# Hybrid attention and MoE block on one core: the first forgetting head's keys, queries and values loaded inside the sliding attention, and five of eight output-weight pieces loaded inside the last forgetting head

## What is computed

```python
def reference(x, meta, ...):
    h = layer_norm(concatenate([meta, x]), ln_in_g, ln_in_b)        # 16 + 2048 tokens, 1024 wide
    proj = h @ w_in                                                 # q,k,v of both head groups, forget gates
    qa, ka, va, qb, kb, vb, fb = split(proj, sizes)
    log_f = log_sigmoid(fb + b_f)
    o_a = sliding_sink_attention(qa, ka, va, sinks, rel_bias, ...)  # 8 heads, 2 key heads, chunks of 64
    o_b = forgetting_attention(qb, kb, vb, log_f, ...)              # 8 heads, causal, bias from cumsum(log_f)
    mix = concatenate([o_a, o_b]) @ w_o
    h = layer_norm(alpha * h + mix, ln1_g, ln1_b)
    h = layer_norm(alpha * h + hierarchical_moe(h, ...), ln2_g, ln2_b)
    return h[:, N_META:]

def forgetting_attention(q, k, v, log_f, key_valid):
    cum = cumsum(log_f)
    for i in blocks of 128 queries:
        s = q_i @ k[:hi].T * HEAD_DIM ** -0.5 + cum_i - cum_keys
        p = softmax(where(causal mask, s, -inf))
        o_i = p @ v[:hi]
```

## Time and profile before

| | us |
|---|---|
| median of three runs | 2511.67 (2507.01 to 2515.30) |
| the profiled execution, its own time | 2511.47 |
| the profiled execution, span from first to last instruction | 2509.5 |
| granted clock of PE, mean over the span | 0.938 of full |
| input projection, from the start to about | 499 |
| sliding attention, about 503 to | 689 |
| forgetting attention, about 695 to | 1267 |
| output projection, from about | 1272 |

### The profile page before, as it was taken

One profiled execution on the slowest core, in us unless ns is written; L12 is line 12 of the kernel. 1 busy time (PEld: TensorE's weight loads), 2 busy tenths in 40 slices (PEclk: granted clock), 3 DMA queues, 4 the chain that ended last, 5 costly groups with the idle time before them and its releaser, 6 DMA issues. The chain is left out here.

```text
span 2509.5 us, 35865 instructions
## 1 busy us (share of the span) xinstructions
PE 2196.5 (88%) x11294; PEld 1790.3 (71%) x11294; DVE 1707.6 (68%) x3144; ACT 1491.3 (59%) x2261; POOL 330.4 (13%) x438
## 2 busy tenths in 40 slices
PE   7999899858859999999979994699999999999970
PEld 6778788645547777777858883587888888788860
DVE  5323231167668888888743334899999999899976
ACT  4323241256557767777633331587888888788856
POOL 0111111110000000000000000122222222222211
PEclk9999999969979999999989996799999999999985
DMA  6525352253252222220043331899787869999837
GB/s 196 175 101 152 126 178 87 76 133 88 64 132 60 66 68 66 68 68 9 8 165 144 142 125 51 294 374 328 240 261 238 281 228 340 325 301 303 270 79 285
DMA packets 213834, 420.06 MB, mean 167 GB/s; under 512 B 42920, under 2 KB 90104, under 8 KB 212824
## 3 DMA queue, kind: packets, MB, share of 16 engines
q1 hardware_dynamic: 180680, 314.15, 36.8%
q0 software_dynamic: 32016, 103.26, 14.3%
q10 hardware_dynamic: 1032, 1.31, 0.4%
HBM read 437.12 MB, written 86.39 MB: 209 GB/s over the span
## 5 line engine op out<-in xcount | busy, mean ns | idle before, releaser
L2348 DVE TENSOR_TENSOR moe_w_lo<-fetch_w_raw,moe_w_hi 128x1024 fp32r<-128x1024 f32 x376 | 435.2, 1217 | 9.4 <-ACT moe_w_hi L2277 9.1
L2277 ACT ACTIVATE moe_w_hi<-fetch_w_raw 128x1024 fp32r<-128x1024 f32 x376 | 368.5, 1053 | 63.9 <-PEq L92 32.5
L2402 PE MATMUL moe_ps_gu<-moe_w_hi,moe_xT_hi 128*128 128x512 f32 x736 | 293.8, 399 | 3.9 <-DVE moe_xT_lo L2359 3.9
L2404 PE MATMUL moe_ps_gu<-moe_w_hi,moe_xT_lo 128*128 128x512 f32 x736 | 289.3, 393 | 0.0
L2403 PE MATMUL moe_ps_gu<-moe_w_lo,moe_xT_hi 128*128 128x512 f32 x736 | 288.7, 392 | 0.0
L1355 ACT ACTIVATE fox_p_hi<-fox_ps_t 128x512 fp32r<-128x512 f32 (+4 forms) x352 | 181.2, 531 | 108.6 <-PE fox_ps_t L1495 107.8
L1422 DVE TENSOR_TENSOR fox_p_lo<-fox_ps_t,fox_p_hi 128x512 fp32r<-128x512 f32 (+4 forms) x352 | 211.0, 611 | 28.7 <-ACT fox_p_hi L1355 27.2
L1495 PE MATMUL fox_ps_t<-ident,fox_s 128*128 128x128 f32 (+1 forms) x1216 | 200.3, 280 | 29.3 <-ACT fox_s L1348 18.4
L2354 DVE TENSOR_TENSOR moe_d_lo<-fetch_d_raw,moe_d_hi 128x1024 fp32r<-128x1024 f32 x184 | 213.1, 1220 | 10.7 <-ACT moe_d_hi L2285 7.4
L1409 DVE CUSTOM_DVE_ANT_0 fox_s<-fox_ps_r,fox_ncum 128x512 f32<-128x512 f32 (+4 forms) x352 | 193.8, 569 | 21.0 <-PE fox_ps_r L1480 13.9
L1348 ACT ACTIVATE fox_s<-fox_s,fox_ntop 128x144 f32<-128x144 f32 (+5 forms) x192 | 173.4, 904 | 46.8 <-DVE fox_ntop L1417 46.3
(11 more groups left out here) (313 smaller groups left out, 4991.4 us busy)
## 6 DMA issues: line engine op xcount, KB each, us to landing
fetch_w_raw<-in_w_e_gate_dram SPq DMA_DIRECT2D x192, 512.0 KB
fetch_w_raw<-in_w_e_up_dram SPq DMA_DIRECT2D x192, 512.0 KB
fetch_d_raw<-in_w_e_down_dram SPq DMA_DIRECT2D x92, 1024.0 KB
proj_w_raw<-in_w_in_dram SPq DMA_DIRECT2D x24, 1024.0 KB, 5.2
proj_xt<-in_x_dram SPq DMA_DIRECT2D x16, 512.0 KB
h<-proj_hrow POOLq DMA_DIRECT2D x16, 512.0 KB, 3.4
win_q_raw<-qT SPq DMA_DIRECT2D x32, 256.0 KB, 4.0
mix_o<-o SPq DMA_DIRECT2D x16, 512.0 KB, 4.4
```

The lines of the kernel that those rows point to most:

```text
L2277: nc.scalar.activation(w_hi[:, k], w_raw[:, k].rearrange("p j n -> p (j n)"), ACT.Copy).then_inc(gu_high, 1)
L2348: nc.vector.tensor_tensor(w_lo[:, k], w_raw[:, k].rearrange("p j n -> p (j n)"), w_hi[:, k].bitcast(F32), ALU.subtract).then_inc(gu_split, 1)
L2402: nc.tensor.matmul(out, xT_hi[:, slot, k], w_hi[:, k, cols], start=k == 0, stop=False)
L2404: done = nc.tensor.matmul(out, xT_lo[:, slot, k], w_hi[:, k, cols], start=False, stop=k == KT - 1)
```

## The change

A tile `raw` of 5200 floats in each partition is made once, outside the four stages, with semaphores `k_in`, `q_in`, `v_in` and `w_in` of its own. In the projection it takes the place of `w_raw` and `gain`; in the forgetting attention it is `k_raw`, `q_raw` and `v_raw`; afterwards its first 5120 floats hold pieces 0 to 4 of `w_o`. `phase_mix` has a smaller tile `w_rest` for pieces 5 to 7. The small tiles of `keep` are made earlier; the instructions on them are the same.

```diff
+RAW = TOK + SEQ + (TILES + 1) * HD
+W_AHEAD = RAW // D
+def load_head(sp, t, ahead, h):
+    k_raw, q_raw, v_raw = raw_head(ahead)
+    row, first = (A_KV + h) * HD, SBT + META
+    for i, cols in enumerate((slice(0, first), slice(first, TOK))):
+        for half in range(2):
+            sp.dma_start(k_raw[half * HD:half * HD + HD, cols], t["kT"][row:row + HD, cols]).then_inc(ahead["k_in"][i], 16)
+    row = (A_HEADS + h) * HD
+    for i, cols in enumerate((slice(0, SBT), slice(SBT, SEQ))):
+        for half in range(2):
+            sp.dma_start(q_raw[half * HD:half * HD + HD, cols], t["qT"][row:row + HD, cols]).then_inc(ahead["q_in"][i], 16)
+    cols = slice((A_KV + h) * HD, (A_KV + h + 1) * HD)
+    sp.dma_start(v_raw[:, 0:TILES], t["v"][META:TOK, cols].rearrange("(b p) d -> p b d", p=P)).then_inc(ahead["v_in"], 16)
+    sp.dma_start(v_raw[0:META, TILES], t["v"][0:META, cols]).then_inc(ahead["v_in"], 16)
...
 # phase_window, SP and POOL
             for n in range(4, TILES):
                 load_queries(n)
                 load_values(n)
+                if n == 11:
+                    sp.wait_ge(fox_zeroed, 1)
+                    load_head(sp, t, ahead, 0)
...
+            nc.gpsimd.memset(raw_head(ahead)[2][:, TILES], 0.0).then_inc(fox_zeroed, 1)
...
 # phase_forget, SP and POOL
-            load_keys(0, K_COLS[0], 0)
-            load_queries(0, Q_COLS[0], 0)
             sp.dma_start(ncum[:, 0, 0:FIRST], row_broadcast(t["ncum"][0, 0:FIRST], P)).then_inc(cum_first, 16)
-            sp.wait_ge(zeroed, 1)
-            load_values(0)
-            load_keys(0, slice(FIRST, TOK), 1)
-            load_queries(0, slice(SBT, SEQ), 1)
             sp.dma_start(ncum[:, 0, FIRST:TOK], row_broadcast(t["ncum"][0, FIRST:TOK], P)).then_inc(cum_in[0], 16)
...
+            sp.wait_ge(k_split, PIECES * B_HEADS)
+            sp.wait_ge(q_split, PIECES * B_HEADS)
+            sp.wait_ge(v_split, 2 * B_HEADS)
+            for k in range(W_AHEAD):
+                sp.dma_start(ahead["raw"][:, k * D:(k + 1) * D], t["w_o"][0, k * P:(k + 1) * P, :]).then_inc(ahead["w_in"][k], 16)
...
-            nc.gpsimd.memset(v_raw[:, TILES], 0.0).then_inc(zeroed, 1)
...
 # phase_mix, SP
-            for k in range(KT):
-                sp.dma_start(w_raw[:, k], t["w_o"][0, k * P:(k + 1) * P, :]).then_inc(w_in[k], 16)
+            for k in range(W_AHEAD, KT):
+                sp.dma_start(w_raw(k), t["w_o"][0, k * P:(k + 1) * P, :]).then_inc(w_in[k], 16)
```

More of the change, by code:

```diff
@@ L100, in row_broadcast, with phase_project @@
     return bass.AP(ap.tensor, ap.offset, [[0, parts]] + [list(x) for x in ap.ap])
-def phase_project(nc, sems, ident, t, gates):
+def phase_project(nc, sems, ident, t, gates, ahead):
     with ExitStack() as ctx:
@@ L116, in phase_project @@
         SLOTS = 6
-        gain = m.sb("gain", [P, D])
+        gain = ahead["raw"][:, 2 * KT * GW:2 * KT * GW + D]
         shift = m.sb("shift", [P, D])
@@ L129, in phase_project @@
         mT = m.sb("mT", [P, KT, 2 * META], F32R)
-        w_raw = m.sb("w_raw", [P, 2, KT * GW])
+        w_raw = ahead["raw"][:, 0:2 * KT * GW].rearrange("p (s n) -> p s n", s=2)
         w_hi = m.sb("w_hi", [P, 2, KT, GW], F32R)
@@ L686, in bucket_runs, with raw_head, phase_window @@
     return runs
-def phase_window(nc, sems, ident, t, gates):
+def raw_head(ahead):
+    raw = ahead["raw"]
+    return raw[:, 0:TOK], raw[:, TOK:TOK + SEQ], raw[:, TOK + SEQ:RAW].rearrange("p (b d) -> p b d", d=HD)
+def load_head(sp, t, ahead, h):
[11 more added lines that the diff above has]
+    sp.dma_start(v_raw[0:META, TILES], t["v"][0:META, cols]).then_inc(ahead["v_in"], 16)
+def phase_window(nc, sems, ident, t, gates, ahead):
     with ExitStack() as ctx:
@@ L744, in phase_window @@
         ones_ready = m.sem("ones_ready")
+        fox_zeroed = m.sem("fox_zeroed")
         k_in = [m.sem(f"k_in{i}") for i in range(2)]
@@ L1119, in row_pieces, with phase_forget @@
     return [(0, keys)] if keys <= 8 * P + META else [(0, half), (half, keys - half)]
-def phase_forget(nc, sems, ident, t):
+def phase_forget(nc, sems, ident, t, ahead):
     with ExitStack() as ctx:
@@ L1190, in phase_forget @@
         ps_o = m.ps("ps_o", [P, 512])
-        zeroed = m.sem("zeroed")
         future_ready = m.sem("future_ready")
@@ L1197, in phase_forget @@
         cum_in = [m.sem(f"cum_in{i}") for i in range(2)]
-        k_in = [m.sem(f"k_in{i}") for i in range(2)]
-        q_in = [m.sem(f"q_in{i}") for i in range(2)]
-        v_in = m.sem("v_in")
+        k_in, q_in, v_in = ahead["k_in"], ahead["q_in"], ahead["v_in"]
         k_high = m.sem("k_high")
@@ L1533, in _, with phase_mix @@
             turn_back(UNITS - 1)
-def phase_mix(nc, sems, ident, t, logits):
+def phase_mix(nc, sems, ident, t, logits, ahead):
     with ExitStack() as ctx:
@@ L1548, in phase_mix @@
         shift = m.sb("shift", [P, D])
-        w_raw = m.sb("w_raw", [P, KT, D])
+        w_rest = m.sb("w_rest", [P, KT - W_AHEAD, D])
         w_hi = m.sb("w_hi", [P, KT, D], F32R)
@@ L1575, in phase_mix @@
         eps_ready = m.sem("eps_ready")
-        w_in = [m.sem(f"w_in{k}") for k in range(KT)]
+        w_in = ahead["w_in"]
         w_high = m.sem("w_high")
@@ L1599, in phase_mix, with w_raw @@
         block = ctx.enter_context(nc.Block())
+        def w_raw(k):
+            return ahead["raw"][:, k * D:(k + 1) * D] if k < W_AHEAD else w_rest[:, k - W_AHEAD]
         def tiles(engine, body):
@@ L1695, in _ @@
                 act.wait_ge(w_in[k], 16)
-                nc.scalar.activation(w_hi[:, k], w_raw[:, k], ACT.Copy).then_inc(w_high, 1)
+                nc.scalar.activation(w_hi[:, k], w_raw(k), ACT.Copy).then_inc(w_high, 1)
             def body(n, slot, use):
@@ L1743, in _ @@
                 dve.wait_ge(w_high, k + 1)
-                nc.vector.tensor_tensor(w_lo[:, k], w_raw[:, k], w_hi[:, k].bitcast(F32), ALU.subtract).then_inc(w_split, 1)
+                nc.vector.tensor_tensor(w_lo[:, k], w_raw(k), w_hi[:, k].bitcast(F32), ALU.subtract).then_inc(w_split, 1)
             dve.wait_ge(norm_in, 32)
@@ L2546, in hybrid_block_kernel @@
         ident = ctx.enter_context(nc.sbuf_tensor("ident", [P, P], F32))
[L2547 to L2553, removed]
         keep = Space(nc, ctx, "keep", ctx)
@@ L2562, in hybrid_block_kernel @@
                  "more_pairs": keep.sb("more_pairs", [1, 1], I32)}
-        phase_mix(nc, ctx, ident, t, logits)
-        with ExitStack() as ahead:
-            raw = Space(nc, ahead, "fetch", ctx)
+        with ExitStack() as before:
+            early_raw = Space(nc, before, "ahead", ctx)
+            ahead = {"raw": early_raw.sb("raw", [P, RAW]),
+                     "k_in": [early_raw.pool_dma_sem(f"k_in{i}") for i in range(2)],
+                     "q_in": [early_raw.pool_dma_sem(f"q_in{i}") for i in range(2)],
+                     "v_in": early_raw.pool_dma_sem("v_in"),
+                     "w_in": [early_raw.pool_dma_sem(f"w_in{k}") for k in range(KT)]}
+            with ExitStack() as early:
+                gate_rows = Space(nc, early, "gates", ctx)
+                gates = {"forget": gate_rows.sb("forget", [B_HEADS, TOK]), "b_forget": gate_rows.sb("b_forget", [B_HEADS, 1]),
+                         "one": gate_rows.sb("one", [B_HEADS, 1])}
+                phase_project(nc, ctx, ident, t, gates, ahead)
+                phase_window(nc, ctx, ident, t, gates, ahead)
+            phase_forget(nc, ctx, ident, t, ahead)
+            phase_mix(nc, ctx, ident, t, logits, ahead)
+        with ExitStack() as fetched:
+            raw = Space(nc, fetched, "fetch", ctx)
             fetch = {"w_raw": raw.sb("w_raw", [P, KT, 2, D_EXPERT]), "d_raw": raw.sb("d_raw", [P, DT, D]),
```

4 lines of the change are left out of this document (1 added, 3 removed).

## The result

| | before | after |
|---|---|---|
| median of 20 runs each, us | 2513.18 (2507.01 to 2516.44) | 2518.57 (2511.61 to 2523.86) |
| ratio after / before | | 1.0020, 95% interval 1.0012 to 1.0029 |
| span of the profiled execution | 2509.5 | 2515.0 |
| granted clock of PE, mean | 0.938 | 0.939 |

The changed kernel is slower by 5.4 us (the interval is 3.0 to 7.3 us). The forecast was 4.8 us slower, and less than the 0.3% from which it would have called the kernel slower. Both came true.

The account below looks back on a forecast made before the run. Stages run one behind another with barriers; in the sliding attention PE is busy 27.58 of 30 us. 2511.47 + 12.7 - 7.6 - 0.3 = 2516.3 us, 2512 to 2519 from the terms' ends, range 2508 to 2522.

Parts of the forecast that it names:

- Part 1, the stall: Sliding attention: ten loads ahead of queries 12 make ACT's split of them 11.0 us late; they land at 636.5.
- the fixed 2.3: Sliding attention, in the landing time of queries 12: 2.3 us that a first small load needs beyond its bytes.
- the store's 1.1: Sliding attention, in the landing time of queries 12: 1.1 us for one 256 KB store of `o` by POOL.
- Part 1, behind the stall: Sliding attention after the stall: loop absorbs 0.3 us; PE at 1.2 GHz for 4.5 to 5 us costs 2.0 us.
- Part 2, the start of the forgetting attention: Forgetting attention's start: PE begins 3.3 us earlier, DVE's waits of 1.40 and 2.88 us go; 7.6 us saved.
- the fourth rival: Forgetting attention's start: `ncum` or a barrier takes the place of keys and queries; 3.3 us lost, 2519.6 us; chance 0.07.
- the upper end of the term: Forgetting attention's start: 9.5 us saved if PE's clock rises earlier because the gap in its work is shorter.
- Part 3, the weights: Five weight pieces loaded during head 7 cost nothing; output projection saves 0.3 us at `o` of tile 2.
- Fast transfers: Sliding attention: loads move at 412 GB/s, queries 12 are 5.2 us late; 2510.0 us; chance 0.15.
- Queries 12 beside the head: Sliding attention: queries 12 are served beside the head's loads, so the stall could vanish; 2503.6 us; chance 0.05.
- The clock that stays down: Sliding attention: PE stays at half clock for 20 us more after the stall, costing 9 us; 2525 us; chance 0.15.
- The sign on later stages: Changed profile: the forecast is wrong if the later stages differ by more than 2 us.

Follow-up runs that it names:

- e1: Changed kernel with head 0's ten loads behind the values of tile 15 instead of tile 11; 2503.73 us against 2512.20 before, ratio 0.9969.
- e4: Changed kernel with only head 0's keys behind values 11, its queries and values behind values 15; one run, 2504.19 us against 2512.20 before.
- e5: Changed kernel with head 0's keys and queries behind values 11, its values behind values 15; one run, 2506.97 us against 2513.82 before.
- e10: Changed kernel with head 0's loads on POOL's queue, behind the store of tile 6, instead of SP's; one run, 2509.61 us against 2511.89 before.
- e8: Changed kernel with head 0's loads on POOL's queue, behind the store of tile 7, instead of SP's; one run, 2512.92 us against 2513.82 before.
- e6: Changed kernel with head 0's loads between queries 12 and values 12 in SP's queue; one run, 2513.45 us against 2513.82 before.
- e7: Changed kernel with head 0's keys behind queries 11, queries behind queries 12, values behind queries 13; 2501.21 us against 2513.82 before, ratio 0.9952.
- e9: e7 with all eight output-weight pieces loaded in the output projection again; 2505.58 us against 2511.89 before, ratio 0.9976.

## Why the prediction was right, point by point

**Part 1, the stall.** Forecast 11.0 us late, measured 12.3. The mechanism was the named one, bytes in front of queries 12 (e1, e4, e5), and the term was 1.3 us too small, inside its ends. The steps of e4, e5 and after show where the 1.3 us are. At my 235 GB/s the keys, the queries and the values are 4.5, 4.5 and 2.2 us, and my other terms (the fixed 2.3 and the store's 1.1 against what queries 12 needed before) take 0.2 off; measured were 5.8, 4.6 and 1.9. So, read from one profile each, the rate was about right and the fixed part too small by 1.5 us, already with the keys alone. The hold of SP by the last value load, 6.66 us, was in no term, though the earlier trace rows has one of 5.32. Because of it queries 12 were issued 12.8 us behind the values and not the 8 to 12 forecast; no cost of it is seen, since the step with the hold in it is the one that came out cheaper than its bytes.

**Part 1, behind the stall.** Forecast -0.3 absorbed and +2.0 for the clock, so +1.7; measured 13.1 - 12.3 = +0.8. The half clock lasted 4.6 us, in the forecast's 4.5 to 5. But the next interval was only 0.93 us longer than before (9.41 against 8.48): the loop, whose tile body is not all PE work, took up more than half of what PE lost. The two errors nearly cancel, and that is luck: 12.7 forecast, 13.1 measured.

**Part 2, the start of the forgetting attention.** Forecast 7.6 us, measured 8.35 (F, 578.56 to 570.21); the nine other kernels with the head ahead have 567.8 to 572.3 in F, the two without it 578.5 and 579.9. PE's first product came 3.5 us sooner (3.3 forecast), and the two waits of DVE (4.3 us) went. The wait for `ncum` that the fourth rival named did appear, with 1.31 us, but it ended what DVE would mostly have waited for PE anyway: at DVE's first scores 3.4 us were saved. The rest of 0.7 fits the clock, which came back after 14 us of PE's work instead of 20; the upper end of the term had that, but no run isolates it.

**Part 3, the weights.** Forecast 0.3 us. In the profile 0.7 us came at tile 2's `o`, as named, and up to 1.5 us in O, of which the kernels with and without it show 0.8 on average. The chip's ratio cannot tell it from 0.

**The rivals.** Fast transfers: at 412 GB/s, by that rival's own sum, after would have been 5.2 us late and not 12.3. The Trainium skill, DMA: Bandwidth & Descriptors, section Bandwidth, gives 341 GB/s for 1 MB over 128 partitions; of the stretches behind 621 one of 2 us reaches that (627 to 629), and 228 and 278 are what the loads cost queries 12. Queries 12 beside the head: no, neither on the same queue (e5) nor on another (e10). The clock that stays down: it came back after 4.6 us of work. A barrier or `ncum` in the place of keys and queries: no, PE's first product came 3.5 us sooner.

**The sign on later stages.** The forecast was to be wrong if the later stages differed by more than 2 us. They differ by 2.2 us in the two profiles, so that sign, taken at its word, was given. But it could not decide anything: the expert stage alone scatters by 8 us among twelve profiles of unchanged code.

**The total.** Up to the last router row the account comes to +3.3 us in the profiles (13.1 - 8.35 - 1.4), against the 4.8 forecast; the medians of 20 runs say 5.4, with an interval that reaches down to 3.0. That 4.8 lies so near to 5.4 is in part luck. The span from the ends of the terms was also given too narrow: the ends as they stand add up to 2510 to 2519.8, not 2512 to 2519.

## What to carry to other kernels

A prefetch is placed by the load that must land next behind it, not by the mean share of the DMA engines: with 64% of the DMA engines' time idle around this place, the same bytes made the kernel 5 us slower than before in one position, 8 us faster at the end of the queue, behind the last urgent load, and 12 us faster when spread over three positions (the last two are not told apart). Divide the bytes by the rate that loads of the same shape show (230 to 280 GB/s here, not the best rate in the profile), compare that with the time until the next urgent load must be there, and cut the prefetch into pieces that fit in between, or put it behind the last urgent load if its own deadline allows. Moving it to another engine's queue is no substitute: look at the time from issue to use of the small load.

## What the hardware showed that I had not expected

**Another queue does not protect a small load.** 256 KB on SP's queue took 4.7 us from issue to use in the kernel before, 10.1 us behind 2.1 MB on the same queue (e5), and 12.9 and 14.7 us beside 2.6 MB on POOL's queue (e8, e10). The Trainium skill, DMA: Bandwidth & Descriptors, section Queues, rings and completion order, says that each DMA engine goes round the queues it has work for, a packet at a time. With even turns, as an estimate from the rates above, 256 KB would have gone with half of 230 GB/s, in 2.3 us plus the fixed part, not in 14.7. That section gives turns by packets and not by bytes, so what the runs contradict is the even turns of the estimate. The Trainium skill, DMA: Bandwidth & Descriptors, section Issuing engines are not separate DMA queues, says that another issuing engine saves only issue time, and with that the runs agree: from the head's first load to the use of the queries it is 17.3 and 19.0 us with POOL, 17.9 and 19.1 with SP. Why the queries came so late was not isolated: the key loads have rows of 2 and 6 KB and the queries rows of 512 bytes, and no run changes the rows or uses the queue of a third engine.

**A load of 4 KB can hold its issuing engine.** It held SP for 6.66 us in after, 6.62 in e6 and 7.68 in e1, for 2.30 us in e7 and 3.74 in e9, where the values stood alone, and for 1.20 us with head 1's values at 717.08, where the earlier trace rows has 5.32. On POOL, in e8 and e10, the same load took 0.53 and 0.54 us to issue. It follows directly on the head's 512 KB of values in rows of 256 bytes, and it was longest where keys and queries were still moving in front of them. What is limited there, I did not isolate.
